# A two-layer hybrid encoder trunk in one core: output stage, first loads and second projections rearranged

## The reference

```python
def rmsnorm(x, g):
    y = x32 * lax.rsqrt(jnp.mean(x32 * x32, axis=-1, keepdims=True) + RMS_EPS)
    return y.astype(x.dtype) * g

def gqa_attention(h, w_qkv, q_norm, k_norm, w_o):
    proj = h @ w_qkv
    ...
    q = apply_axial_rope(rmsnorm(q, q_norm), tables) * (GQA_HEAD_DIM ** -0.5)
    k = apply_axial_rope(rmsnorm(kv[:, :, 0], k_norm), tables)
    v = kv[:, :, 1]
    ...
    return jnp.concatenate([out_meta, out_real], axis=1) @ w_o

def reference(x, meta_tokens, ...):
    h = jnp.concatenate([meta, x], axis=1)
    for i in range(DEPTH):                       # DEPTH = 2
        u = rmsnorm(h, norm_mix[i])
        mix = neighbourhood_attention(u, ...) if i == 0 else gqa_attention(u, ...)
        h = h + mix
        h = h + swiglu(rmsnorm(h, norm_ffn[i]), ffn_w1[i], ffn_w3[i], ffn_w2[i])
    return rmsnorm(h, norm_final)[:, N_META:]
```

## Time and profile before

| | us |
|---|---|
| median of 3 runs | 2985.32 (2982.59 to 2988.23) |
| the profiled execution, its own time | 2982.6 |
| its span | 2980.7 |
| mean granted clock | 0.972 of full speed |

### The profile page before, as it was taken

How to read it: one execution, slowest core, us unless ns; L and a number is a source line. 1 busy time by engine, 2 the same in 40 slices (tenths; PEclk the granted TensorE clock), 3 DMA queues, 4 the chain that set the end, 5 groups by cost and what they waited for, 6 DMA issues and landing times.

```text
span 2980.7 us, 39897 instructions
## 1 busy us (share of the span) xinstructions
PE 2816.1 (94%) x15091; PEld 2300.8 (77%) x15091; DVE 1283.9 (43%) x1659; ACT 654.8 (22%) x1123; POOL 1366.0 (46%) x1399
## 2 busy tenths in 40 slices
PE   5999999899999999999898999996999999999993
PEld 5888887799999999999675444443778888888882
DVE  3444445352222222225767566664342222233235
ACT  3333333311000000002123445543210000000001
POOL 3665556344444444445335455643444444444440
PEclk8999999999999999999998999998999999999996
DMA  7221222311111111112321000002111111111111
GB/s 191 61 74 56 62 69 94 140 46 40 47 47 49 48 47 47 47 46 88 91 64 36 1 15 1 15 15 116 51 46 50 46 48 44 45 46 49 50 43 58
DMA packets 227508, 166.17 MB, mean 56 GB/s; under 512 B 24936, under 2 KB 209680, under 8 KB 227232
## 3 DMA queue, kind: packets, MB, share of 16 engines
q1 hardware_dynamic: 219408, 136.17, 16.3%
q10 hardware_dynamic: 7952, 27.89, 2.5%
HBM read 133.19 MB, written 26.03 MB: 53 GB/s over the span
## 4 chain that ended last, share of the span: by engine, by line
PE 81%; DVE 9%; issue 3%; DMA 3%; SPq 1%; ACT 1%; POOL 1%; ACTq 0%; DVEq 0%; POOLq 0%
PE PS L686 58%; PE PS L812 8%; PE PS L1076 3%; PE PS L1090 2%; DVE nmx L1862 2%; PE PS L863 2%; PE PS L899 2%; PE PS L839 2%; DVE rcp L1891 2%; PE PS L1016 1%; DMA wraw<-in_a_w_qkv 1%; DMA out<-fin 1%; DVE accd L1878 1%; PE PS L961 1%; DVE ssq L1486 1%
## 5 line engine op out<-in xcount | busy, mean ns | idle before, releaser
L498 POOL TENSOR_TENSOR wh<-wraw,ones 128x512 fp32r<-128x512 f32 (+1 forms) x456 | 417.0, 914 | 1232.1 <-PE PS L686 1040.4
L501 POOL TENSOR_TENSOR wl<-wraw,wh 128x512 fp32r<-128x512 f32 (+1 forms) x456 | 521.4, 1143 | 35.8
L686 PE MATMUL PS<-uh,wh 128*128 128x348 f32 (+1 forms) x1696 | 453.8, 363 | 20.5 <-POOL wl L501 8.2
L686 PE MATMUL PS<-uh,wl 128*128 128x348 f32 (+1 forms) x1696 | 446.9, 359 | 0.0
L686 PE MATMUL PS<-ul,wh 128*128 128x348 f32 (+1 forms) x1696 | 446.7, 358 | 0.0
L1527 DVE TENSOR_TENSOR h<-PS,h 128x1044 f32<-128x1044 f32 (+1 forms) x192 | 236.8, 1234 | 333.6 <-PE PS L686 318.8
L686 PEld LDWEIGHTS PS<-uh,wh 128*128 128x128 f32 x1696 | 302.5, 190 | 77.6 <-issue 31.1
L686 PEld LDWEIGHTS PS<-ul,wh 128*128 128x128 f32 x1696 | 305.2, 190 | 38.1
L686 PEld LDWEIGHTS PS<-uh,wl 128*128 128x128 f32 x1696 | 304.2, 189 | 36.1
L1191 ACT ACTIVATE at<-at 128x1044 f32<-128x1044 f32 (+1 forms) x44 | 47.1, 1069 | 864.6 <-DVE at L1539 864.6
L686 PE MATMUL PS<-yh,wh 128*128 128x348 f32 x1056 | 225.5, 322 | 5.0 <-DVE h L1527 3.0
(11 more groups left out here) (222 smaller groups left out, 4029.8 us busy)
## 6 DMA issues: line engine op xcount, KB each, us to landing
wraw<-in_ffn_w SPq DMA_DIRECT2D x176, 256.0 KB, 2.9
wraw<-in_ffn_w SPq DMA_DIRECT2D x176, 128.0 KB, 2.2
wraw<-in_a_w_qkv SPq DMA_DIRECT2D x48, 256.0 KB, 2.9
biasb<-bias_rows SPq DMA_DIRECT2D x128, 72.0 KB, 2.7
h<-h_spill ACTq DMA_DIRECT2D x16, 522.0 KB, 9.2
h_spill<-h SPq DMA_DIRECT2D x8, 522.0 KB, 6.4
h_spill<-h ACTq DMA_DIRECT2D x8, 522.0 KB, 3.0
xt<-in_x SPq DMA_DIRECT2D x8, 512.0 KB, 12.3
```

Of the source, the lines that this page charges most:

```text
L498: nc.gpsimd.tensor_tensor(wh[:, slot, 0:w], wraw[:, slot, 0:w], ones[:, 0:1].to_broadcast([P, w]), ALU.mult).then_inc(s_whi, 1)
L501: nc.gpsimd.tensor_tensor(wl[:, slot, 0:w], wraw[:, slot, 0:w], wh[:, slot, 0:w].bitcast(F32), ALU.subtract).then_inc(s_wrd, 1)
L686: mm = nc.tensor.matmul(PS[:, set_ + c, 0:cw], w, x[k][:, c * cw:(c + 1) * cw], start=(first and i == 0 and ti == 0), stop=(last and i == ...
```

## The change

Output stage: the gain is applied by ACT into a buffer of its own, `hg`, one piece at a time, as the last projection's pieces are added. The squares are summed per token with eight matmuls against one column of ones, so the reciprocal root works on 8 columns. The factor is applied per partition as the transposed tiles are copied. Four pairs of banks and four buffers `fin` are used instead of one and two, a tile is every other token of 256 (`tile_tokens`), and a store has 16 grid rows of 8 columns as its outer dimensions, where it had 8 rows of 16.

First loads: an x tile is all 16 rows of 8 columns. The gains are transposed behind tile 5, their copy stands ahead of tile 6. The fill of `bias_rows` is issued behind the fifth square. The 16 copies of the relative bias are issued by ACT behind its first high parts, and SP asks for the first v weights ahead of the bias loads.

Second projections: the norm vectors are loaded right behind mask and meta bias and scaled on DVE ahead of the first output projection. `scale_v` stands one item later, behind the second `scale_chunk`, `L0_AT` is moved by one item at two places. The clears of `vg` and `zero_odd` stand ahead of the split of the first output weights, which goes to step 8 of block 0. PE's wait for the rounded identity goes to its first use. The late spreads go from steps 5 and 7 to 6 and 8.

```diff
+OUTS = 4
+F_BANK = [(6, 7), (5, 2), (0, 1), (3, 4)]
-L0_AT = [6, 7, 7, 8, 8]
+L0_AT = [7, 7, 8, 8, 8]
...
+        def tile_tokens(i):
+
+            return bass.ds(2 * P * (i // 2) + i % 2, P, step=2)
...
@@ sync @@
             for i in range(8):
                 sp.dma_start(xt[:, i, :],
-                             x_g[i % 2, :, CB * (i // 2):CB * (i // 2) + CB, :]
-                             .rearrange("r c d -> c r d")).then_inc(s_xl[i], 16)
+                             x_g[:, HR * i:HR * i + HR, :]).then_inc(s_xl[i], 16)
...
-            sp.wait_ge(s_bfill, 16)
-            for c in range(CB):
-                sp.dma_start(bias_rows[:, c, 4:19, c + 1:c + 32], A["a_rel_bias"][0],
-                             allow_slow_non_contiguous=True).then_inc(s_brow, 16)
+            fetch_chunk(4, w_qkv, 2 * D)
             load_bias(0)
-            fetch_chunk(4, w_qkv, 2 * D)
...
-                sp.dma_start(out_g[i % 2, :, CB * (i // 2):CB * (i // 2) + CB, :],
-                             fin[:, i % 2, :]).then_inc(s_out[i % 2], 16)
+                sp.dma_start(out_g[:, CB * (i // 2):CB * (i // 2) + CB, :]
+                             .rearrange("r (c z) d -> z r c d", z=2)[i % 2],
+                             fin[:, i % OUTS, :]).then_inc(s_out[i % OUTS], 16)
@@ gpsimd @@
-            split_pair(U_WO[1], U_WO[1] // 2)
             po.wait_ge(s_un, U_GQ + 2 * ITEMS)
...
+                    if n == 0 and kt == KT - 1:
+                        split_pair(U_WO[1], U_WO[1] // 2)
@@ tensor @@
-                if kt in (5, 7):
-                    half = (kt - 5) // 2
+                if kt in (6, 8):
+                    half = (kt - 6) // 2
...
-            pe.wait_ge(s_idr, 1)
...
                 if i == 4:
+                    pe.wait_ge(s_idr, 1)
                     pe.wait_ge(s_vgh, 3)
...
-            stat(4)
+            pe.wait_ge(s_ssq, 4)
+            pe.wait_ge(s_df, G_FF[1] + 132)
             for i in range(8):
-                pe.wait_ge(s_fs, KC * (i // 4 + 1))
+                mm = nc.tensor.matmul(PS[:, 4, i:i + 1], ssq[:, tile_tokens(i)], ones[:, 0:1],
+                                      start=True, stop=True)
+            mm.then_inc(s_st, 1)
+            pe.wait_ge(s_hg, KC)
+            for i in range(8):
+                if i == 3:
+                    pe.wait_ge(s_fv, 1)
+                if i >= 4:
+                    pe.wait_ge(s_fca, i - 3)
+                    pe.wait_ge(s_fcb, i - 3)
                 for f in range(2):
-                    if i:
-                        pe.wait_ge(s_fcb if f else s_fca, i)
                     for c in range(4):
-                        mm = nc.tensor.transpose(PS[:, 6 + f, P * c:P * c + P],
-                                                 h[:, 4 * f + c, P * i:P * i + P], ident[:, :])
+                        mm = nc.tensor.transpose(PS[:, F_BANK[i % 4][f], P * c:P * c + P],
+                                                 hg[:, 4 * f + c, tile_tokens(i)], ident[:, :])
@@ scalar @@
+                if k == 4:
+                    nc.scalar.activation(hg[:, m, :], h[:, m, 0:GRID], ACT.Copy,
+                                         scale=gains[:, 4, m:m + 1]).then_inc(s_hg, 1)
...
+            act.wait_ge(s_bfill, 16)
+            for c in range(CB):
+                act.dma_start(bias_rows[:, c, 4:19, c + 1:c + 32], A["a_rel_bias"][0],
+                              allow_slow_non_contiguous=True).then_inc(s_brow, 16)
             act.wait_ge(s_ur, KC)
             act.wait_ge(s_hsp, 16 * KC)
...
+            nc.scalar.activation(sst[:, 8:9], ones[:, 0:1], ACT.Sqrt).then_inc(s_rt, 1)
+            act.wait_ge(s_fv, 1)
+            nc.scalar.activation(ssy[:, 0:8], ssv[:, 0:8], ACT.Sqrt).then_inc(s_rt, 1)
...
-                nc.scalar.activation(fin[:, i % 2, 0:512], PS[:, 6, :], ACT.Copy).then_inc(s_fca, 1)
+                nc.scalar.activation(fin[:, i % OUTS, 0:512], PS[:, F_BANK[i % 4][0], :], ACT.Copy,
+                                     scale=ssv[:, i:i + 1]).then_inc(s_fca, 1)
@@ vector @@
+            dve.wait_ge(s_gc2, 48)
+            nc.vector.tensor_scalar(gnb[:, 0:1], gnb[:, 0:1], HD ** -0.5, None, ALU.mult).then_inc(s_gnb, 1)
+            nc.vector.memset(gnb[64:P, 1:2], 1.0).then_inc(s_gnb, 1)
             proj_out(0)
             ffn(0)
...
-            dve.wait_ge(s_gc2, 48)
-            nc.vector.tensor_scalar(gnb[:, 0:1], gnb[:, 0:1], HD ** -0.5, None, ALU.mult).then_inc(s_gnb, 1)
-            nc.vector.memset(gnb[64:P, 1:2], 1.0).then_inc(s_gnb, 1)
...
                 rope(i - 1)
-                if c == 0:
-                    scale_v(g - 1)
                 if g and c == 1:
                     scale_chunk(g - 1, 0)
+                    scale_v(g - 1)
...
-            for half in (slice(0, GRID // 2), slice(GRID // 2, GRID)):
-                for m in range(KC):
-                    nc.vector.scalar_tensor_tensor(h[:, m, half], h[:, m, half], gains[:, 4, m:m + 1],
-                                                   rstd[:, half], op0=ALU.mult,
-                                                   op1=ALU.mult).then_inc(s_fs, 1)
```

97 lines of the change are left out of this document (59 added, 38 removed).

## The result

The changed kernel takes 2906.1 us in the median of four runs (2903.6 to 2907.8), beside 2984.2 (2982.6 to 2988.2) for the kernel before on the same chip: a ratio of 0.9737 (95% interval 0.9725 to 0.9749). The forecast was 2905, range 2890 to 2923. The profiled execution took 2904.7 us with a span of 2902.9, 77.8 less than the 2980.7 of before; its mean granted clock is 0.986 instead of 0.972, and PE is busy for 2795.3 us, 96% of the span.

The account below looks back on a forecast made before the run. TensorE carries most of the chain, so only its waits and low clock stretches can give time back. Terms 9 + 6.0 + 8.6 + 5.0 + 10 + 41.5 = 80.1 us off the 2985.32 median give 2905 us, range 2890 to 2923.

Parts of the forecast that it names:

- the prediction's own signs: Trace marks: v projection from 63.5, blocks 1 to 3 near 29 us, end 22 to 24; wrong if first fill after 80.
- First loads: Start: x tiles land earlier, bias row fill goes behind the fifth tile, same bytes pass; 0, between -1 and +1.5 us.
- Bias rows to ACT: Start: copies on ACT's queue let SP fetch the v chunk sooner, projection follows scores at once; -9 us (-3 to -11).
- Rival 3: Start: bias rows, mask and meta bias share one queue, land 6 us later; gain only 3, 2911 us; chance 0.10 (alone or with rival 2).
- Norm vectors: Second projections, layer one: ACT copies item 0 earlier, PE waits 2.2 us instead of 7.4; -6.0 us (-4 to -7).
- `scale_v` later: Second projections: `take_sums` ends before PE asks in groups one and two, 0.4 wait in three; -8.6 us (-5 to -9.5).
- Clears: Change over to attention: POOL clears ahead of the weight split, so the row spread comes 4.2 us earlier; -5.0 us (-3 to -7).
- Late spreads: Attention blocks 1 to 3: the 1.48 us wait and slow clock go, 87.0 us instead of 97.9; -10 us (-4 to -12).
- Rival 2: Middle gives little: late spreads 3, `scale_v` 4, so 11.6 us less gain, 2917 us; chance 0.13.
- Output stage: End: short statistic, transposes meanwhile, stores at 359 to 400 GB/s on all engines; -41.5 us (-27 to -44).
- rival 1: End: stores stay at half the engines, 160 GB/s; the end gives 27 instead of 41.5, 2920 us; chance 0.12.
- Rival 4: End: each store spread over only two engines, 105 us for the stores; slower by 13, 2998 us; chance 0.02.

Follow-up runs that it names:

- experiment 2: Changed kernel with the 16 relative bias copies back on SP behind the spill, ahead of bias loads and first v chunk: 2914.2 us, ratio 0.9771 to the kernel before.

## Why the prediction was right, and where its steps failed

The total came out 1.1 us above the forecast, which is better than its terms were. By the traces the gain is 77.8 us, where the sum has 80.1. Eight of the nine lines of the table are within 3 us. The start lacks 7.2 and the output stage 2.9; six small surpluses, 7.8 together, hide most of that, and that they do is luck. By the prediction's own signs the start was wrong: the first fill came at 84.4, later than its 80, and the v projection began at 71.4 instead of 63.5. The end took 25.4 us instead of 22 to 24. The signs of the middle came true, but for the 2 us of waiting before the first head sums, which are gone altogether.

*First loads, 0.* Wrong: beside the old place of the copies they cost about 5 us (experiment 2). I looked at the bytes on the DMA engines, and not at what DVE does once the tiles are there earlier. DVE then meets POOL's splits, the slot of the weights comes free later, and the spill and everything behind it on SP with it.

*Bias rows to ACT, -9.* The move gave 6.7. The step that failed is "ACT is through with its first high parts at 37.2": its queue issues a DMA while high parts before it still run (the last four until 34.9), so the copies go out from 30.5, ahead of the spill at 33.99, and "most of the traffic is over by then" did not hold. `take_q` waits 9.36 us for the spill, and the scores slip by 8.5 us, where I allowed 0.5, up to 3; 2.5 of these are the low clock behind the wait, for which I had no term. Rival 3 named the right number, 3 us for the start at most, by another way: not the mask and the meta bias land late (62 against 55, and still ahead of `take_k`), but the spill does. With the spill moved, the forecast time of the first filler is met to 0.2 us.

*Norm vectors, -6.0.* Right in kind, 7.9 measured and 9.4 by undoing, so somewhat too small. I let ACT copy item 0 at 1436.0 and kept a wait of 2.2 us. In fact ACT squares it at 1430.2 already, and PE, which waited 7.40 us, does not wait at all.

*`scale_v` later, -8.6.* 8.7 and, undone, 8.6. DVE's 0.65 us in group two were enough. The rule of the Trainium skill on DVE and POOL ("SBUF — State Buffer", "Who interferes with whom"), by which it would have been 1 us less, did not show in this sum.

*Clears, -5.0.* 6.6 both ways.

*Late spreads, -10.* The difference of the two profiles is 10.0, but undoing the part gives 6.8. One profile of before showed the clock falling behind the wait in each block; other runs of the same middle show 3 us less. The step took a consequence that comes in some runs for a part of the wait, so that its 10.0 came out exactly is in part luck. Rival 2, 3 us, was too low all the same.

*Output stage, -41.5.* 38.6 and, alone, 39.0. Engines and rate were right (358 GB/s, share 0.98), and rival 1 falls, as does the 341 GB/s of the Trainium skill ("DMA: Bandwidth & Descriptors", "Bandwidth"), by which, as an estimate, it would have been 1 us less; the measurement decides. Of the 2.9 us that are missing, 1.2 are the sums (3.36 for 2.2). PE has idled 3.78 us and does them at the low clock, which I had charged to two tiles of transposes only; my bound of 2.83 was that of four wide matmuls at a clock of 0.68. I had also counted eight loads, and the trace has 16. The other 1.8 are in the stores, which I let run at full rate from their issue on. From the first issue to the end it takes 15.6 us, where 13.8 were taken: nothing moves in the first microsecond, and 111 and 176 GB/s in the next two.

*Second SwiGLU block.* A term that was missing, -3.0, of which the 32 bytes explain 1.9.

Rival 4 falls with the stores.

## What to carry to other kernels

A DMA moved to an idle queue is not free: look at which transfers are in flight when it now starts, and at who waits for those; many short rows took 177 of 321 GB/s from a spill that nobody had waited for. Count the low clock behind a new wait as well: it made 6.0 us into 8.5. When a step becomes quicker, ask first which engine then starts earlier and what it meets, as DVE met POOL here. And when a wait is costed from one profile, keep the low clock behind it apart from the wait itself: the first is there every time, the second is not, and now and then the low clock comes without it.

## What the runs showed of the hardware that was not expected

- The same idle time of PE, 1.47 and 1.48 us at the same instruction, was followed once by the high and once by the low clock; the difference was 3 us in a block of 30. In two blocks of 27 the clock fell behind 0.47 and 0.50 us, at 1.6 us each.
- A store of 512 KB with 8 outer rows reached 210 GB/s at a share of 0.51 with four buffers in flight, and 152 with two; with 16 outer rows it was 358 with four and 235 to 262 with two.
- Moving `uh`, `ul`, `h` and all that lies behind them by 32 bytes in SBUF came with 1.7 to 1.9 us less for 3144 matmuls, about 0.25%, in one trace, with the order of instructions unchanged. Whether it is the moving or the stationary operand was not tried.
- 16 one column matmuls, each with its own 128 by 128 load, take 3.36 to 3.58 us at a clock of 0.50 to 0.55, 2.74 at 0.70 and 2.04 at 1.00.
